# A two-layer hybrid diffusion block on one core: the second layer's modulation summed by VectorE inside the merges instead of by TensorE in the opening

## The reference

```python
for l in range(DEPTH):
    mod_lat = (jax.nn.silu(c) @ w_ada[l] + b_ada[l])[:, None, :]     # 1024 -> 3*1024
    mod_ctx = jax.nn.silu(c_ctx) @ w_ada[l] + b_ada[l]
    u_c, gate_c = adaln_modulate(h_ctx, mod_ctx)    # layer_norm(h) * (1 + scale) + shift, gate
    u_x, gate_x = adaln_modulate(h_lat, mod_lat)
    pc, px = split_proj(u_c @ w_in[l]), split_proj(u_x @ w_in[l])
    ya = gated_delta_net(...); yb = hyena(...); yc = gqa(...); yd = differential_attention(...)
    out = merge_branches((ya, yb, yc, yd), merge_logits, w_br[l], w_out[l])
    #     = sum over n of sigmoid(logits[n]) * (y[n] @ w_br[l][n]), then @ w_out[l]
    h = layer_norm(ALPHA * h + gate * out) * ln_g[l] + ln_b[l]
```

## Time and profile before

| | |
|---|---|
| runs | 2765.77, 2761.46, 2755.30 us |
| median | 2761.46 us |
| profiled execution, its span | 2761.2 us |
| TensorE busy | 2632.7 us, 95% |
| VectorE busy | 1542.8 us, 56% |
| ScalarE busy | 947.1 us, 34% |
| GpSimd busy | 560.8 us, 20% |
| data moved by DMA | 250.97 MB, mean 91 GB/s |
| opening of layer 1 | 1561.2 to 1657.2, 96.0 us |

### The profile page before, as it was taken

The page is one execution under the profiler, slowest core; times in us unless marked ns, Lnnn a source line. Parts: engine busy times, 40 slices in busy tenths (PEclk is TensorE's granted clock), DMA queues, the critical chain, the costliest instruction groups (busy, mean ns, idle before and its releaser), DMA issues.

```text
span 2761.2 us, 50245 instructions
## 1 busy us (share of the span) xinstructions
PE 2632.7 (95%) x21342; PEld 2268.3 (82%) x21342; DVE 1542.8 (56%) x2752; ACT 947.1 (34%) x1498; POOL 560.8 (20%) x232
## 2 busy tenths in 40 slices
PE   7899999999999999999999989899999999999998
PEld 1399888899999999997897538888778788888776
DVE  5755777427654443434647764668738643352656
ACT  0335333322322343224532233443343334433541
POOL 0122000120113211321023502200131132242032
PEclk9999999999999999999999999999999999999999
DMA  7421000332222112220134552100153331332033
GB/s 251 160 75 48 16 30 24 110 117 97 81 89 90 61 54 102 79 91 33 34 120 150 192 197 78 47 26 26 42 181 109 113 106 53 109 115 69 24 122 115
DMA packets 95165, 250.97 MB, mean 91 GB/s; under 512 B 11010, under 2 KB 32516, under 8 KB 94432
## 3 DMA queue, kind: packets, MB, share of 16 engines
q1 hardware_dynamic: 84170, 219.56, 23.9%
q10 hardware_dynamic: 10774, 28.19, 2.9%
HBM read 205.12 MB, written 35.26 MB: 87 GB/s over the span
## 4 chain that ended last, share of the span: by engine, by line
PE 84%; DVE 8%; ACT 3%; issue 2%; DMA 2%; SPq 0%; ACTq 0%; DVEq 0%
PE ps L1012 19%; PE ps L1014 19%; PE ps L1013 19%; PE ps L1020 6%; PE ps L1029 3%; PE ps L1041 2%; PE ps L1638 2%; PE ps L1152 2%; PE ps L1669 2%; PE ps L1652 2%; PE ps L1666 2%; PE ps L1198 1%; DVE t_gcv L2366 1%; PE ps L1106 1%; DMA t_raw<-in_w_ada 1%
## 5 line engine op out<-in xcount | busy, mean ns | idle before, releaser
L973 POOL TENSOR_TENSOR t_wlo<-t_raw,t_whi 128x1024 fp32r<-128x1024 f32 x217 | 534.1, 2462 | 2125.9 <-ACT t_whi L1775 2125.8
L1012 PE MATMUL ps<-t_u_hi,t_whi 128*128 128x384 f32 (+1 forms) x2368 | 845.5, 357 | 17.6 <-ACT t_oT L1846 6.7
L1014 PE MATMUL ps<-t_u_hi,t_wlo 128*128 128x384 f32 (+1 forms) x2368 | 825.9, 349 | 0.0
L1013 PE MATMUL ps<-t_u_lo,t_whi 128*128 128x384 f32 (+1 forms) x2368 | 825.1, 348 | 0.0
L1775 ACT ACTIVATE t_whi<-t_raw 128x1024 fp32r<-128x1024 f32 x235 | 248.3, 1057 | 773.9 <-PE ps L1014 704.7
L1012 PEld LDWEIGHTS ps<-t_u_hi,t_whi 128*128 128x128 f32 x2368 | 445.8, 188 | 52.7 <-issue 19.5
L1014 PEld LDWEIGHTS ps<-t_u_hi,t_wlo 128*128 128x128 f32 x2368 | 445.3, 188 | 23.7
L1013 PEld LDWEIGHTS ps<-t_u_lo,t_whi 128*128 128x128 f32 x2368 | 446.3, 188 | 21.0 <-issue 0.5
L1846 ACT ACTIVATE t_grp<-ps 128x256 f32<-128x256 f32 (+2 forms) x192 | 80.6, 435 | 232.5 <-PE ps L1029 134.5
L1012 PE MATMUL ps<-t_b_hi,t_whi 128*128 128x384 f32 (+1 forms) x384 | 137.7, 358 | 6.3 <-DVE t_acc L2358 3.4
L2366 DVE SCALAR_TENSOR_TENSOR t_gcv<-ps,t_par,t_gcv 128x128 f32<-128x128 f32 (+8 forms) x192 | 84.8, 494 | 98.0 <-ACT t_gcv L1846 96.2
(11 more groups left out here) (322 smaller groups left out, 3926.7 us busy)
## 6 DMA issues: line engine op xcount, KB each, us to landing
t_raw<-in_w_in SPq DMA_DIRECT2D x184, 512.0 KB, 3.6
t_raw<-in_w_ada SPq DMA_DIRECT2D x48, 512.0 KB, 4.5
t_raw<-in_w_br SPq DMA_DIRECT2D x32, 512.0 KB, 3.8
t_raw<-in_w_out SPq DMA_DIRECT2D x24, 512.0 KB, 3.8
t_sg<-gate_logits SPq DMA_DIRECT2D x28, 384.0 KB, 4.3
hs<-t_hstage ACTq DMA_DIRECT2D x20, 512.0 KB, 4.5
t_hring<-hs SPq DMA_DIRECT2D x20, 512.0 KB, 6.1
t_prob<-t_pT ACTq DMA_DIRECT2D x56, 128.0 KB, 2.1
```

The costliest lines, as they stand in the source:

```text
L973: pool.tensor_tensor(lo, raw[:, s % RAW, :], hi.bitcast(f32), ALU.subtract)\
L1012: pe.matmul(o, lh, rh, start=first, stop=False)
L1013: pe.matmul(o, lh, rl, start=False, stop=False)
L1014: return pe.matmul(o, ll, rh, start=False, stop=last)
```

## The change

In layer 1 the 24 `ada` steps, the four `turn` steps, the bias loads and the rows that VectorE adds up leave the opening, and its other steps are put in another order. The chunks of layer 1 are summed in six merges instead, one chunk each: chunks 0 to 3 in the four merges of layer 0, chunks 4 and 5 in merges (1,1) and (1,2). SP loads each `w_ada` piece into one new buffer, `mraw`, outside the stream; from the second piece on it waits for `md_used`, VectorE's release of the piece before. VectorE multiplies each 128 by 512 half of a piece by a per-partition scalar of `cs` and adds it to `msum`, once for each of the two rows (in layer 1's merges for the latent row alone). After the fourth piece TensorE sums over partitions: with `msum` as the stationary side and a column of ones (eight one-column fp32 matmuls) for chunks 0 to 3, or with `pick` as the stationary side and `msum` moving (one matmul of 512 columns) for chunks 4 and 5. VectorE adds the bias. Layer 0's modulation is computed as before. The diff, cut:

```diff
@@ -153,62 +157,13 @@ (opening, layer 1)
-    for q in range(4):
-        yield "ada", 0, q
-        if q % 2:
-            yield "sum", 3 + q // 2, 0
...
-    for q in range(4):
-        yield "ada", 5, q
...
+    yield from (("sum", 3, 0), ("tap", 0, 0), ("sum", 4, 0), ("nrm", 3, 0), ("tap", 0, 1), ("sum", 5, 0))
+    yield from (("nrm", 4, 0), ("gain", 3, 0), ("tap", 0, 2), ("nrm", 5, 0), ("gain", 4, 0), ("stat", 0, 0))
+    yield from (("tap", 0, 3), ("gain", 5, 0), ("stat", 1, 0), ("tap", 1, 0), ("stat", 2, 0), ("tap", 1, 1))
+    yield from (("stat", 3, 0), ("stat", 4, 0), ("blk", 0, 0), ("tap", 1, 2), ("stat", 5, 0), ("blk", 0, 1))
+    yield from (("tap", 1, 3), ("unit", 0, 0), ("put", 0, 0), ("unit", 1, 0), ("blk", 0, 2), ("unit", 2, 0))
+    yield from (("unit", 3, 0), ("put", 0, 1), ("unit", 4, 0), ("unit", 5, 0), ("blk", 1, 0), ("u", 0, 0))
+    yield from (("blk", 1, 1), ("u", 1, 0), ("put", 1, 0), ("blk", 1, 2), ("u", 2, 0), ("u", 3, 0), ("put", 1, 1))
@@ (SP)
+            def modulation_piece(coming):
+                for L, a, b in coming:
+                    q = chunks_loaded[0]
+                    chunks_loaded[0] += 1
+                    if q:
+                        sp.wait_ge(sems["md_used"], q)
+                    x = A["w_ada"][L, a, b].rearrange("p (k c) -> p k c", k=2)
+                    sp.dma_start(mraw[:, :, :], x).then_inc(bada_ld[0], 16)
+                    return
             def gate_loads(l, n):
+                coming = iter([(L, a, b) for L, a in SUMMED_IN.get((l, n), ()) for b in range(4)])
...
+                modulation_piece(coming)
...
                     pieces(1 if d >= x else 0)
+                    if 4 <= d < 7:
+                        modulation_piece(coming)
@@ (TensorE)
+            def across_partitions(L, a, bank):
+                summed_chunks[0] += 1
+                pe.wait_ge(sems["ada_row"], OPEN_CHUNKS + summed_chunks[0])
+                claim(bank)
+                rows = summed_rows(L, a)
+                if a < GATE_CHUNK:
+                    for j in range(4):
+                        for v in rows:
+                            last = pe.matmul(ps[:, bank, 2 * j + v:2 * j + v + 1], msum[:, v, j * P:(j + 1) * P],
+                                             ones[:, 0:1], start=True, stop=True)
+                else:
+                    for v in rows:
+                        last = pe.matmul(ps[0:2, bank, :], pick[:, v:v + 2], msum[:, v, :],
+                                         start=v == 0, stop=v == rows[-1])
...
                 project(full, "mg_sg")
+                chunks = SUMMED_IN.get((l, n), ())
+                for L, a in chunks:
+                    across_partitions(L, a, 7)
                 ln.take("mg_y", BT)
@@ (ScalarE, in the step put)
-                        splits_due()
+                        if l or a == 3:
+                            splits_due()
@@ (VectorE)
+            def add_piece(L, a, b):
+                dve.wait_ge(bada_ld[0], 16 * (macs[0] + 1 + OPEN_CHUNKS // 2))
+                macs[0] += 1
+                for k in range(2):
+                    for v in summed_rows(L, a):
+                        x, y, c = mraw[:, k, :], msum[:, v, :], cs[:, 2 * b + k, v:v + 1]
+                        if b == 0 and k == 0:
+                            ins = ts(y, x, c, None, ALU.mult)
+                        else:
+                            ins = stt(y, x, c, y, ALU.mult, ALU.add)
+                    ln.step(ins, "md_used" if k else "dve_step")
+                if b == 3:
+                    ln.done(dve.drain(), "ada_row")
...
                     ln.step(tt(b_lo[:, j, 0:w], yv[:, 0:w], b_hi[:, j, 0:w].bitcast(f32), ALU.subtract), "mg_y")
+                    for L, a in chunks:
+                        add_piece(L, a, j)
```

More of the change, by code:

```diff
@@ L437, in trunk @@
         cs = sb("cs", [P, KT, 2])
+        bcol = sb("bcol", [P, 16])
+        pick = sb("pick", [P, 4])
         oT = sb("oT", [P, BT, TOK])
@@ L543, in trunk @@
             sil_s = sb("sil_s", [P, max(SCAN_SILU), TOK], stack=m)
+            mraw = sb("mraw", [P, 2, 512], stack=m)
+            msum = sb("msum", [P, 2, 512], stack=m)
         with ExitStack() as m:
@@ L686, in trunk, with summed_rows @@
         SCAN_PHASES = NT * 11
+        def summed_rows(L, a):
+            return (0, 1) if a < GATE_CHUNK or L == 0 else (0,)
         def gate_units(l):
@@ L831, in silu_loads @@
                     sp.dma_start(sil_s[:, j, 0:w], logits[l, 0, KT + j, :, 0:w]).then_inc(sems["ld_c"], 16)
-            def gate_loads(l, n):
+            chunks_loaded = [0]
+            def modulation_piece(coming):
[7 more added lines that the diff above has]
+                    return
+            def gate_loads(l, n):
+                coming = iter([(L, a, b) for L, a in SUMMED_IN.get((l, n), ()) for b in range(4)])
+                if l == 0 and n == 0:
+                    x = A["b_ada"][1][0:1, 0:2 * D].rearrange("a (j p) -> p (a j)", p=P)
+                    sp.dma_start(bcol[:, :], x, allow_slow_non_contiguous=True).then_inc(bada_ld[1], 16)
+                for L, a in SUMMED_IN.get((l, n), ()):
+                    if a >= GATE_CHUNK:
+                        c = (a - GATE_CHUNK) * 512
+                        x = A["b_ada"][L][:, a * 512:(a + 1) * 512]
+                        sp.dma_start(grow[:, c:c + 512], x).then_inc(bada_ld[1], 16)
+                modulation_piece(coming)
                 stored_by(stored[0])
@@ L864, in open_loads @@
                         parity_table(fctab, "ld_c")
-                    if kind == "ada" and (a, b) == ((2, 0) if l else (3, 0)):
-                        if l:
-                            sp.wait_ge(sems["wo_h"], NT)
+                    if kind == "ada" and (a, b) == (3, 0):
                         class_table(ftab, "ld_ftab")
@@ L2468, in open_layer @@
                 g = groups(l)
+                if l == 0:
+                    step(dve.memset(pick[:, :], 1.0))
+                    step(dve.memset(pick[:, 1:2], 0.0))
                 dve.wait_ge(sems["ld_par"], 256 if l else 96)
@@ L2830, in out_norm, with summed_out, merge @@
                     ln.done(tt(x, x, r, ALU.mult), "on_x")
-            def merge(l, first, last=False):
+            macs, rows_out = [0], [0]
+            def add_piece(L, a, b):
[11 more added lines that the diff above has]
+                    ln.done(dve.drain(), "ada_row")
+            def summed_out(L, a, bank):
+                ln.take("ada_t")
+                if a >= GATE_CHUNK:
+                    rows_out[0] += 1
+                    dve.wait_ge(bada_ld[1], 16 * (rows_out[0] + 1 + OPEN_CHUNKS // 2))
+                    c = slice((a - GATE_CHUNK) * 512, (a - GATE_CHUNK + 1) * 512)
+                    ln.done(tt(grow[:, c], ps[0:2, bank, :], grow[:, c], ALU.add), "ada_mod")
+                    return
+                if a == 0:
+                    dve.wait_ge(bada_ld[1], 16 * (1 + OPEN_CHUNKS // 2))
+                t = ps[:, bank, 0:8].rearrange("p (j r) -> p j r", r=2)
+                b = bcol[:, 4 * a:4 * a + 4].unsqueeze(2).broadcast_to([P, 4, 2])
+                if a < 2:
+                    ln.done(tt(mod[:, 4 * a:4 * a + 4, :], t, b, ALU.add), "ada_mod")
+                else:
+                    ln.done(stt(mod[:, 4 * a:4 * a + 4, :], t, 1.0, b, ALU.add, ALU.add), "ada_mod")
+            def merge(l, n):
+                first, last = n == 0, n == 3
+                chunks = SUMMED_IN.get((l, n), ())
                 w = width(l == 0)
@@ L3146, in _ @@
                 fence(ln, "dve")
-                merge(l, True)
+                merge(l, 0)
                 fence(ln, "dve")
@@ L3150, in _ @@
                 fence(ln, "dve")
-                merge(l, False)
+                merge(l, 1)
                 fence(ln, "dve")
@@ L3154, in _ @@
                 fence(ln, "dve")
-                merge(l, False)
+                merge(l, 2)
                 fence(ln, "dve")
@@ L3159, in _ @@
                 fence(ln, "dve")
-                merge(l, False, True)
+                merge(l, 3)
                 fence(ln, "dve")
```

79 lines of the change are left out of this document (20 added, 59 removed).

## The result

The changed kernel takes **2827.26 us** (median of four runs, 2823.36 to 2831.40), the kernel before 2758.38 beside it (2751.28 to 2765.77). The ratio is 1.0246 with a 95% interval of 1.0228 to 1.0263: slower by 69 us. The forecast was 2803 us in a range of 2770 to 2826. The sign and the place were right, the size was too small by 24 us, and the time lies just outside the range.

What follows compares the result with a forecast made beforehand. The prediction took TensorE, busy 95% of the span, to bound the kernel. Opening -14, layer 0's merges +38, merges (1,1) and (1,2) +16, the rest +2 gave +42 on 2761.2: 2803 us, range 2770 to 2826.

Steps and rivals of the forecast that it cites:

- part 4: Six merges: the first `mraw` load ahead of `sg` and `raw` loads costs some tenths each, 2 us, between 0 and 6.
- The bound and the ceiling: Whole kernel: TensorE bounds it; in layer 1's opening VectorE is next, so the gain there ends at 32 us.
- The chain followed: Layer 1's opening: VectorE's 62.4 us of work plus 14.8 us waiting on TensorE's blocks, 77.2 us.
- The opening's gain: Layer 1's opening falls from 96 to 82 us, a gain of 14 us, between 6 and 32.
- 1 us for VectorE working beside GpSimd: Layer 1's opening: an allowance of 1 us added for VectorE working beside GpSimd.
- The clock: Layer 1's opening: between one and two TensorE blocks run at the lower clock after idle time, 4 us.
- The wait of layer 0's merges: Merges (0,0) to (0,3): TensorE waits 6.0 us in each for the fourth piece's sum, between 3.1 and 6.5.
- What stands behind the wait: Layer 0's merges: one-column matmuls 2.2 us and the branch's start at the lower clock 1.4 us, in each.
- Merges (1,1) and (1,2): Each costs 8.2 us: wait 5.5, matmul on `msum` 1.3, lower clock 1.4; 16 us for both.
- case D: Six merges: the single buffer's chain slips a whole piece, waits about 10 us each; about 2825 us, chance 0.12.
- A: The forecast: TensorE waits 4 to 7 us for the sum in each of six merges; 2785 to 2820, chance 0.66.
- Layer 0's opening: Some high parts are made later but nothing waits for them: 0, plus or minus 0.5 us.

Runs made afterwards that it cites:

- kept_busy: gpsimd_late plus 24 unused fp32 matmuls in TensorE's gaps in layer 1's opening: 2812.79 us.
- gpsimd_late: Changed kernel, with GpSimd converting layer 1's first three pieces only after VectorE's fold of the second filter's row: 2817.04 us.
- two_buffers: Changed kernel with a second buffer for `w_ada` pieces and the second to fourth pieces loaded one raw piece earlier: 2785.46 us.
- late_reader: Changed kernel with the matmuls on `msum` moved from ahead of the branch to ahead of its last `w_br` piece, except in merge (0,3): 2786.49 us.
- busy_wait: Changed kernel with six unused fp32 matmuls of 512 columns ahead of TensorE's wait for `msum` in each of the six merges: 2807.61 us.
- first_behind: two_buffers with a merge's first `w_ada` piece loaded behind the third tile's raw piece, not at the head of its loads: 2777.46 us.
- no_sums: Changed kernel with the second layer's modulation left out (its loads, multiply-adds and matmuls), so the new opening alone: 2752.44 us.
- opening_best: no_sums plus GpSimd's late conversions (as in gpsimd_late) and the filler matmuls in layer 1's opening (as in kept_busy): 2747.23 us.
- old_order: no_sums with the opening's remaining steps in the order of the kernel before: 2749.78 us.

## Why the prediction was wrong, step by step

The spans differ by 68.4 us where 42 were forecast. Of the 26 us between, 5 are the opening's, 11 those of layer 0's merges, 8 those of merges (1,1) and (1,2) with part 4, and 2 lie elsewhere. The mechanism and the place were right; three terms were too small.

- **The bound and the ceiling were right.** TensorE bounds the merges, and VectorE is next in the opening. The chain followed gave 77.2 us, and kept_busy, with the two disturbances removed, is 77.0 to the first projection matmul, or 78.5 to the later end that the forecast used. VectorE's work there is 60.4 us, 60.9 forecast for the same stretch.
- **The opening's gain: 14 forecast, 8.8 measured.** The step that failed here is the "1 us for VectorE working beside GpSimd". It measured 7.1 (85.65 to 78.6 in gpsimd_late). I had left out that three conversions move with the loads. The clock, put at 4 us, is worth 1.6 (kept_busy); the two errors partly cancelled, which was luck.
- **The wait of layer 0's merges: 6.0 forecast, 6.3 measured** (25.1 in four), by the chain that was told: collision, release, issue, landing, additions. two_buffers and late_reader show that its lateness is the price. The multiply-adds took 737 ns at the least and 2777 at the most. That agrees with the Trainium skill ("GPSIMD Engine Reference", section 1), by which GpSimd's SBUF interfaces contend with a VectorE instruction of two SBUF inputs. The same row of it names instructions in a 2-port mode. The fold's last row has one SBUF input, takes 0.42 us alone, and took 2.45 beside GpSimd; that would fit, but no view says in which mode it ran.
- **What stands behind the wait was mis-sized, and this is the larger part of the error in layer 0.** The sixteen records took 3.4 us (865.82 to 869.25), not 2.2, and the branch 35.8 us instead of 33.6 on average, 2.2 more and not 1.4. With the wait that is 11.9 a merge, 48 for four where 38 were forecast (48.6 from span to span). The 2.2 had no row behind it: 1.7 us slowed as in the earlier trace rows gives 2.7, and as in the earlier trace rows 3.1. The 1.7 itself was right, for the records took 1.8 us in late_reader. busy_wait confirms the records' share, late_reader the branch's.
- **Merges (1,1) and (1,2): 16 forecast, 26 measured.** The wait was 6.7 on average, 5.5 forecast, the matmul on `msum` 1.8 and not 1.3, and the branches 1.4 longer, as forecast: 20 us for the two. The other 6 are the step that failed, part 4, the `w_ada` load ahead of the raw loads: I priced it at tenths of a microsecond a merge. In (1,1) it cost a wait of 3.1 us and slow tiles behind it, and first_behind takes most of this wait away. In layer 0, with tiles of 8.3 us, it didn't show on TensorE. That VectorE's own wait for a piece holds up `b_lo` was missed too; it is hidden behind the wait for `msum` until the reader moves (late_reader).
- **Left open:** the 6.9 us between the opening and the end of merge (1,0). No instruction there is changed. The same stretch took 381.5 us in no_sums, 389.6 in opening_best and in old_order, which have no sums either, 385.7 in the kernel before and 392.6 in the changed kernel. Kernels that do the same there thus lie 8 us apart, and 4.8 of the 6.9 are pauses of TensorE for which the profile names no releaser ("issue", 11.0 us instead of 6.2). That it is chance isn't shown.
- **The range.** Its upper end counted errors of the wait alone (case D). The terms behind the wait and the collision in the opening have one sign and came together. D's own terms give 2821, not the 2825 that it states, and although the measured time lies near them, its mechanism didn't happen: no wait for `msum` was longer than 6.9 us, where D has about 10. What came is A with dearer terms. Layer 0's opening (0 forecast) was right: the first projection began at 136.5 us in both traces.

## What to carry to other kernels

A wait put in front of the bounding engine is paid more than once: here 6.3 us as idle time, and some 3.8 us again in the slower matmuls behind it. Price both, or take the wait away; filler work gave back only part. A load chained through one buffer is as late as the sum of release, issue, landing and use, so ask for the last piece of the chain whether its reader can stand later, and what else stands behind it in the list of the engine that sums. When work leaves a queue, follow what moves up in its place: here three conversions moved up onto a row that had never met them.

## What the runs showed of the hardware

- A VectorE instruction on one partition, 1x512 with one SBUF input and a scalar, took 2.45 us beside a GpSimd subtraction and 0.42 without it. I had looked for collisions at two-input instructions alone.
- A one-column fp32 matmul is far from free: sixteen records took 3.4 us behind idle time (352 ns each, overlapped) and 1.8 us where TensorE had been busy (250 ns each). Each loads 128x128 weights, 333 and 192 ns a record at the median; that this load sets the price is likely but wasn't tried.
- Six useless matmuls ahead of each of six waits made this program 20 us faster by the medians; the traces place 11 us of that at the waits.
